# Two tiles of tokens through all heads, then the other two, in the last stage of a two-layer kernel

## The reference

```python
def _peer(h, wq, keys, u, v):                       # P_HEADS 8, P_TOPK 16, N_KEYS 128
    def block(xt):                                  # 128 tokens
        q = (xt @ wq).reshape(P_BLOCK, P_HEADS, 2, P_HALF)
        s = jnp.einsum('nhpd,hpkd->nhpk', q, keys)
        s1, i1 = lax.top_k(s[:, :, 0], P_TOPK)
        s2, i2 = lax.top_k(s[:, :, 1], P_TOPK)
        ...                                         # the 16 best of the 256 sums, idx = i1*128 + i2
        g = jax.nn.softmax(top_s.astype(jnp.float32), axis=-1)...
        act = jax.nn.gelu(jnp.einsum('nd,ned->ne', xt, u[idx]), approximate=False)
        return jnp.einsum('ne,ned->nd', g * act, v[idx])
```

## Time and profile before

| | |
|---|---|
| median of 3 runs | 4204.72 us (4201.19 to 4205.2) |
| the profiled execution | 4206.81 us, its span 4205.0 us |
| PE busy | 3455.8 us (82%) |
| DVE busy | 1977.0 us (47%) |
| POOL busy | 939.2 us (22%) |
| ACT busy | 657.9 us (16%) |
| moved by DMA | 1157.36 MB, mean 275 GB/s |
| gathers of the last stage | 512, first issued at 2838.4 us, last at 4170.2 us |

### The profile page before, as it was taken

The page is one execution under the profiler, slowest core; times in us unless marked ns, Lnnn a source line. Parts: engine busy times, 40 slices in busy tenths (PEclk is TensorE's granted clock), DMA queues, the critical chain, the costliest instruction groups (busy, mean ns, idle before and its releaser), DMA issues. The chain is left out here.

```text
span 4205.0 us, 37527 instructions
## 1 busy us (share of the span) xinstructions
PE 3455.8 (82%) x11876; PEld 1566.1 (37%) x11877; DVE 1977.0 (47%) x4086; ACT 657.9 (16%) x1532; POOL 939.2 (22%) x811
## 2 busy tenths in 40 slices
PE   7988998497999979998879655578888887887876
PEld 3345443332333323333254344444333333333332
DVE  5824223322332232232252264436666667667676
ACT  1011220000000000000021112212222222221212
POOL 2000000112221220121220040003444444444442
PEclk9999998698999989999989766689899999999998
DMA  9816333579989993888861000027999999999997
GB/s 331 287 72 229 111 102 112 205 277 411 367 347 363 386 412 121 311 333 337 311 233 61 6 1 0 1 80 300 421 418 417 419 408 413 413 409 421 411 421 333
DMA packets 194149, 1157.36 MB, mean 275 GB/s; under 512 B 25659, under 2 KB 27995, under 8 KB 74356
## 3 DMA queue, kind: packets, MB, share of 16 engines
q1 hardware_dynamic: 97140, 565.17, 34.6%
q0 software_dynamic: 80576, 564.05, 32.7%
q10 hardware_dynamic: 16320, 26.75, 2.1%
HBM read 1128.96 MB, written 48.68 MB: 280 GB/s over the span
## 5 line engine op out<-in xcount | busy, mean ns | idle before, releaser
L2167 POOL DMA_INDIRECT q_uv<-in_peer_uv,q_picks x512 | 576.3, 1126 | 1128.0 <-PE ps L2259 709.9
L1149 PE MATMUL ps<-wt,e_xT 128*64 128x512 f32 x3200 | 731.1, 611 | 99.6 <-DMA wt<-in_w_exp 98.7
L2462 DVE SCALAR_TENSOR_TENSOR mod<-q_uv,mix 128x1024 f32<-128x1024 f32 x512 | 627.3, 1225 | 391.1 <-DMA q_uv<-in_peer_uv,q_picks 386.7
L2259 PE MATMUL ps<-q_uv,q_dg 128*128 128x512 f32 x1024 | 512.3, 656 | 135.0 <-ACT q_dg L2336 135.0
L2259 PE MATMUL ps<-q_uv,tri 128*128 128x512 f32 x1024 | 474.0, 618 | 88.1 <-ACT tri L2336 88.0
L1129 POOL COPY wt<-e_land 128x2048 f32<-128x2048 f32 x124 | 237.6, 1916 | 1023.3 <-DMA e_land<-in_w_exp 1023.2
L1149 PEld LDWEIGHTS ps<-wt,e_xT 128*64 128x64 f32 x3200 | 237.7, 141 | 583.2 <-issue 432.2
L1149 PE MATMUL ps<-wt,e_aT 128*64 128x512 f32 x1600 | 356.0, 597 | 21.6 <-ACT e_aT L1202 21.6
L2259 PEld LDWEIGHTS ps<-q_uv,q_dg 128*128 128x128 f32 x1024 | 211.1, 211 | 427.2 <-issue 427.2
L2259 PEld LDWEIGHTS ps<-q_uv,tri 128*128 128x128 f32 x1024 | 198.1, 197 | 360.4 <-issue 360.4
L454 PE MATMUL ps<-hT,wt 128*128 128x512 f32 x640 | 285.0, 602 | 1.5 <-DVE wt L781 1.5
(11 more groups left out here) (439 smaller groups left out, 3483.2 us busy)
## 6 DMA issues: line engine op xcount, KB each, us to landing
wt<-in_w_exp SPq DMA_DIRECT2D x260, 1024.0 KB, 17.6
e_land<-in_w_exp SPq DMA_DIRECT2D x124, 1024.0 KB, 23.5
wt<-in_w_in_units SPq DMA_DIRECT2D x15, 2048.0 KB, 11.4
mod<-in_w_mod_units SPq DMA_DIRECT2D x48, 512.0 KB, 5.7
scratch_xs<-const_zeros SPq DMA_DIRECT2D x8, 2080.0 KB
mod<-in_w_ada_units SPq DMA_DIRECT2D x32, 512.0 KB, 6.1
p_ring<-in_w_in SPq DMA_DIRECT2D x7, 2048.0 KB, 9.6
e_xg<-scratch_xs ACTq DMA_DIRECT2D x104, 128.0 KB
```

The costliest lines, as they stand in the source:

```text
L1149: ins = nc.tensor.matmul(ps[64 * h:64 * h + 64, at, :], lhs[:, k % 4, 64 * (k // 4):64 * (k // 4) + 64], wt[:, u, a, h * W:(h + 1) * W], s ...
L2167: pool.indirect_dma_start(out=uv[:, n % NR, :, :].rearrange("p a d -> p (a d)"), out_offset=None, in_=A["peer_uv"], in_offset=bass.Indirec ...
L2259: last = nc.tensor.matmul(acc(t)[:, c, :], dg(n), uv[:, n % NR, 1, c * W:(c + 1) * W], start=fresh, stop=closing)
L2462: dve.scalar_tensor_tensor(junk[:, n % 2, :], uv[:, n % NR, 0, :], 1.0, mix[:, tile_of(k), :], ALU.mult, ALU.mult, accum_out=ap[:, k % 2, ...
```

## The change

The batches are taken in another order. Tiles 0 and 1 go through all eight heads (batches 0 to 15, the tile alternating), then tiles 2 and 3. There are now 16 rounds `v` of queries, each for one head and two tiles (256 tokens); the weights of head `v % 8` are loaded for each round, so every head's are read twice. A round is one stretch of 16 matmuls of 256 columns in bank 6 after gather 3 of each odd batch, and 4 score matmuls in bank 7 after gather 9. Round 0 is still done tile by tile; round 1 stands ahead of the gathers' matmuls, where tile 2's first queries were. Tiles 2 and 3 are transposed later (`columns`, in batches 2 and 4). Each tile has PSUM banks of its own; tile 3 takes tile 0's once it has been read (`s_tot`). `gather_sum`, `ysum` and `s_ev` are gone; `qT` and `sc` are half as large.

```diff
-ORDER = (0, 2, 1, 3)
+ORDER = (0, 1, 2, 3)
+PAIR = 2
+ROUNDS = PH * NT // PAIR
...
         def tile_of(k):
-            return ORDER[k % NT]
+            return PAIR * (k // (PAIR * PH)) + k % PAIR
 
         def acc(t):
-            return ps[:, 2 * min(t, 2):2 * min(t, 2) + 2, :]
+            return ps[:, 2 * (t % 3):2 * (t % 3) + 2, :]
...
-                for h in range(2, PH):
-                    sp.wait_ge(s_q, NT if h == 2 else q_done(h - 2, 1))
-                    sp.dma_start(wq[:, h % 2].rearrange("p k w -> p (k w)"), A["peer_wq_2_units"][h]).then_inc(s_wq[h % 2], 16)
-                    if h == 2:
+                for v in range(2, ROUNDS):
+                    sp.wait_ge(s_q, q_done(v - 2))
+                    sp.dma_start(wq[:, v % 2].rearrange("p k w -> p (k w)"), A["peer_wq_2_units"][v % PH]).then_inc(s_wq[v % 2], 16)
+                    if v == 2:
                         sp.wait_ge(s_h, NT)
                         sp.dma_start(ln2[:, 0, :], ...).then_inc(s_ln2, 16)
...
+                def queries(v):
+                    t = PAIR * (v // PH)
+                    pe.wait_ge(s_wq[v % 2], 16 * (v // 2 + 1))
+                    pe.wait_ge(s_h, t + PAIR)
+                    pe.wait_ge(s_qe, q_done(v - 1))
+                    if v in (3, 4):
+                        pe.wait_ge(s_tT, NT + 2 * v)
+                    for c in range(2):
+                        for k in range(KD):
+                            last = nc.tensor.matmul(ps[:, 6, c * PAIR * P:(c + 1) * PAIR * P], wq[:, v % 2, k, c * NK:(c + 1) * NK],
+                                                    hT[:, k, t * P:(t + PAIR) * P], start=(k == 0), stop=(k == KD - 1))
+                    last.then_inc(s_q, 1)
...
                 pe.wait_ge(s_mix, 2 * NT)
-                first_queries(2)
+                queries(1)
+                scores(1)
...
-                    if j == 0 and t >= 2 and k >= 2:
-                        pe.wait_ge(s_ev, k // 2)
+                    if j == 0 and k == PAIR * PH + 1:
+                        pe.wait_ge(s_tot, 1)
...
-                    if k == 0 and j == 3:
-                        first_queries(3)
-                    if h + 1 < PH and k % NT == 0 and j in (7, 13):
-                        queries(h + 1, int(j == 13))
-                    if h + 1 < PH and k % NT == 1 and j == 5:
-                        scores(h + 1)
+                    if k in (2, 4) and j == 5:
+                        columns(PAIR + k // 2 - 1)
+                    v = k // PAIR + 2
+                    if k % PAIR == 1 and v < ROUNDS:
+                        if j == 3:
+                            queries(v)
+                        if j == 9:
+                            scores(v)
...   (ScalarE, in batch k, after the diagonals of group g)
-                            if k % NT == 0 and g == 3:
-                                queries(h + 1, 0)
-                            if k % NT == 1 and g == 0:
-                                queries(h + 1, 1)
-                            if k % NT == 1 and g == 2:
-                                scores(h + 1)
+                        if k % PAIR == 1 and v < ROUNDS:
+                            if g == 1:
+                                queries(v)
+                            if g == 3:
+                                scores(v)
...   (VectorE)
-                def gather_sum(k):
-                    ...
-                        if j == 8 and 1 <= k <= last_head and tile_of(k - 1) >= 2:
-                            gather_sum(k - 1)
-                        if k > last_head and j in (6, 8, 10, 12, 14):
+                        if k - 1 in last_of and j in (6, 8, 10, 12, 14):
                             finish(k - 1, (j - 6) // 2)
```

More of the change, by code:

```diff
@@ L2104, in route_peer @@
         s_full, s_mix, s_h, s_q, s_qe, s_sc, s_se = (sem(n) for n in ("full", "mix", "h", "q", "qe", "sc", "se"))
[L2105 removed]
+        s_u, s_v, s_ge, s_w, s_dg, s_tot = (sem(n) for n in ("u", "v", "ge", "w", "dg", "tot"))
         s_uv = [sem(f"uv{i}") for i in range(NR)]
@@ L2114, in tile_of, with q_done, scores_done @@
         def tile_of(k):
-            return ORDER[k % NT]
+            return PAIR * (k // (PAIR * PH)) + k % PAIR
         def acc(t):
-            return ps[:, 2 * min(t, 2):2 * min(t, 2) + 2, :]
[L2122 to L2130, removed]
+            return ps[:, 2 * (t % 3):2 * (t % 3) + 2, :]
+        def q_done(v):
+            return PAIR + v
+        def scores_done(v):
+            return PAIR + v
+        last_of = {PAIR * PH * (t // PAIR + 1) - PAIR + t % PAIR: t for t in range(NT)}
         with nc.Block() as block:
@@ L2206, in first_queries @@
                     for c in range(2):
-                        last = nc.tensor.matmul(ps[:, 7, c * NK:(c + 1) * NK], qT[:, c, t * P:(t + 1) * P], keysT[:, c, :],
+                        last = nc.tensor.matmul(ps[:, 7, c * NK:(c + 1) * NK], qT[:, c, i * P:(i + 1) * P], keysT[:, c, :],
                                                 start=True, stop=True)
                     last.then_inc(s_sc, 1)
[L2211 to L2217, removed]
+                def queries(v):
[9 more added lines that the diff above has]
+                                                    hT[:, k, t * P:(t + PAIR) * P], start=(k == 0), stop=(k == KD - 1))
@@ L2218, in queries, with scores @@
                     last.then_inc(s_q, 1)
-                def scores(h):
-                    pe.wait_ge(s_qe, q_done(h, 1))
-                    for i, t in enumerate(ORDER):
+                def scores(v):
+                    pe.wait_ge(s_qe, q_done(v))
+                    pe.wait_ge(s_se, scores_done(v - 1))
+                    for i in range(PAIR):
                         for c in range(2):
-                            last = nc.tensor.matmul(ps[:, 6 + i // 2, (2 * (i % 2) + c) * NK:(2 * (i % 2) + c + 1) * NK],
-                                                    qT[:, c, t * P:(t + 1) * P], keysT[:, 2 * h + c, :], start=True, stop=True)
+                            last = nc.tensor.matmul(ps[:, 7, (2 * i + c) * NK:(2 * i + c + 1) * NK],
+                                                    qT[:, c, i * P:(i + 1) * P], keysT[:, 2 * (v % PH) + c, :], start=True, stop=True)
@@ L2227, in scores, with columns @@
                     last.then_inc(s_sc, 1)
+                def columns(i):
+                    t = ORDER[i]
+                    pe.wait_ge(s_h, i + 1)
+                    pe.wait_ge(s_tT, NT + 2 * i)
+                    pe.wait_ge(s_qe, q_done(i))
+                    pe.wait_ge(s_se, scores_done(i))
+                    for b in range(2):
+                        for k in range(4):
+                            last = nc.tensor.transpose(ps[:, 6 + b, k * P:(k + 1) * P],
+                                                       mix[:, t, (4 * b + k) * P:(4 * b + k + 1) * P], ident[:, :])
+                        last.then_inc(s_tm, 1)
@@ L2322, in _ @@
                 root(3)
-                first_queries(2)
+                queries(1)
+                scores(1)
                 exponentials(1)
                 for k in range(NBATCH):
-                    h = k // NT
+                    v = k // PAIR + 2
                     for g in range(BATCH // G):
@@ L2397, in choose @@
                 def choose(k, part):
-                    lists = [sc[:, (k // NT) % 2, k % NT, c, :] for c in range(2)]
+                    lists = [sc[:, (k // PAIR) % 2, k % PAIR, c, :] for c in range(2)]
                     settle()
                     if part == 0:
-                        dve.wait_ge(s_se, k + 1 if k < NT else scores_done(k // NT))
+                        dve.wait_ge(s_se, k + 1 if k < PAIR else scores_done(k // PAIR))
                         for c in range(2):
```

74 lines of the change are left out of this document (29 added, 45 removed).

## The result

The changed kernel takes 4211.8 us (median, 4207.16 to 4216.4), the kernel before 4202.57 us on the same chip (4198.59 to 4206.8); 18 runs each, ratio 1.0022 [1.0014, 1.0029]. So it is 9.2 us slower. I had forecast 0.5 us more: the result lies inside the stated range (4196 to 4222), just outside the forecast's own (4200 to 4211), and just beyond the 0.2% (8.4 us) that I had called "no change". The profiled execution took 4212.47 us, with a span of 4210.6 us.

A forecast was written before the change was run, and what follows sets the result against it. It took DMA transfers, full at 421 GB/s between query rounds, to bound the last stage. Terms +12.5 - 11.9 + 1.2 - 1.3 = +0.5 us gave 4207.3 us profiled, median 4205.2; range 4196 to 4222, the forecast's own 4200 to 4211.

The forecast's parts named there:

- step 2: Query bursts in the last stage: loads fill holes in the transfers, idle 8.0 us against 19.9, so -11.9 us.
- My signs: 46 us windows: over 415 GB/s around bursts ending with a load, about 405 around the last two; wrong at 400 or less.
- the second cause: Load and burst's hole add up instead of cancelling; sign: windows around bursts with a load at 400 GB/s or less.
- 1, loads: Last stage's full stretch: 12 weight loads instead of 6, ln2 leaves; net +5 MB at 2.49 us, +12.5 us.
- 3, start: Last stage's start: round 1's queries for two tiles replace tile 2's first, scores later by +1.2 us (bounds -1, +3).
- 4, tail: `gather_sum` goes; only its last instruction stands on the final chain: -1.3 us.
- 5, waits: Waits added for copied scores and queries: cost 0; 7 us if their cover went.
- on top of the hole: After each burst, load and first gathers share engines: 1.65 us more for 12 bursts, +19.8, 4225 us; chance 0.25.
- Evenly spaced bursts hurt no more: All 14 bursts' holes close, idle 0, -8.0 us: 4197 us, 4195 with the start's lower bound; chance 0.13.
- Short matmuls are slower: Query bursts: 16 uncovered weight loads make each 3 us longer, 43 us over 14, at most 4248 us; chance 0.04.

The follow-up runs named there:

- e10: Kernel before with only the changed kernel's start of the last stage, no load more: 4197.44 us beside 4203.85 us, ratio 0.999.
- e1: Kernel before with each query burst from batch 4 on cut into pieces, one behind each group of four gathers: 4206.08 us, before 4204.72 us, ratio 0.9999.
- e2: Changed kernel with each query burst cut into two halves 4 gathers apart: 4213.18 us, ratio to the kernel before 1.0016.
- e8: Kernel before with the second matmul of each gather cut from 512 columns to 2, output half wrong: 4198.6 us, ratio 0.999.
- e9: Kernel before with the second matmul of each gather left out, output half wrong: 4194.03 us, ratio 0.9981.
- e4: Changed kernel with loads from round 4 on issued 16 gathers later, between bursts: 4213.65 us, ratio to the kernel before 1.002.
- e3: Changed kernel without the second reading of query weights (8 loads of 1 MB gone, result not the reference's): 4194.2 us, ratio to the kernel before 0.9971.
- e5: Kernel before with seven more 1 MB loads, each issued as a round's first burst ends: 4218.43 us beside 4202.15 us, ratio 1.004.
- e6: Kernel before with seven more 1 MB loads, each in the middle between rounds of bursts: 4221.49 us beside 4202.15 us, ratio 1.0045.

## Why the prediction was right or wrong, step by step

The number fell into the stated range, but the mechanism on which the forecast stood failed (step 2): the range was wide enough for the result through its rivals, which took the same holes for real, and that is luck. My signs did not tell either: bursts with a load moved 421, 421, 401, 405 and 414 GB/s, partly as forecast and partly as in the second cause.

*1, loads (+12.5 us): right.* 6 loads more in the rounds gave 14.6 us, one MB less ahead of them 2.5 us back: 12.1 us.

*2, bursts (-11.9 us): this step failed.* I had written that TensorE's burst lets the ring run dry, and "a 1 MB load that starts as a burst ends fills the hole which the burst tears". Of the 11.9 us at most the 3.9 us that lie at the start came (dot product 64 is 6.3 us sooner, 2.5 us of that is the MB of ln2; with the changed start alone, in e10, 1.8 us were left); the 8.0 us of the rounds did not. Nothing was torn and nothing filled: the burst can be cut up (e1, e2), TensorE unloaded (e8, e9), the load moved (e4), left out (e3) or added at the burst or far from it (e5, e6), and a round takes 161 to 162 us plus about 2.5 us for each MB. The dips are real in the earlier trace rows, but I read them as time lost against the 421 GB/s of quiet windows. The trace of before has 16 landings for each gather, as many as there are DMA engines, and I take one to be each engine's. These show where the error is. Time of a gather's first landing (us from the span's start): us from it to the last landing:

```
before  3121.5: 2.02   3133.9: 2.99   3183.5: 4.05   3349.3: 5.07   3389.0: 5.16   3588.4: 1.15
after   2904.7: 1.88   3108.5: 3.02   3123.3: 4.01   3183.3: 7.19   3292.9: 6.40   3349.1: 8.55
```

Between 3121 and 3134 us, with two packets of the instruction queues at 3126.7 (queue 8) and 3127.0 (queue 14), the spread goes up by 1 us and stays. In a quiet stretch it grows to 5 us, while 421 GB/s are moved, and most of it is the very last landing (at 3349.3 us the 15th comes 2.4 us behind the first, the 16th 5.1): the other engines run ahead into the ring's slack, and one falls behind. When the ring is thin they wait for it, and the window shows a dip. In the changed kernel, with no dip for 400 us, the spread grew to over 6 us (over 8 around a load), and the dips then came without bursts. So a quiet window shows more than the lasting rate, and a dip shows what was run ahead.

What sets the lasting rate can be read from the last landings alone. In e9, where it is clearest, the last landing of a gather comes 2.485 us (median) behind that of the gather before. Besides the loads and stores, the delays of over 0.5 us from gather 64 on are 20 steps of 0.89 to 0.99 us, each beside a packet of queue 14:

```
gathers       64-128     128-192      192-256      256-320      320-384      384-448  448-511
steps at      74 98 118  140 163 184  207 230 250  274 294 318  339 360 384  406 426  450 470 498
```

64 x 2.485 = 159.0 us, three steps of 0.96 and a load of 2.5 are 164.4 us (measured 164.4 to 164.7), three steps without a load 161.9 (162.0), two steps 161.0 (161.1). So what a round takes beyond the bytes of its gathers and loads is two or three such steps. They stand beside 20 of the 29 packets of queue 14 in these rounds, which last only 0.325 us; beside the other 9 there is no delay. In the kernel before the steps are nearly the same, a few of them beside a packet of queue 8 alone (at 3435.6 and 3823.8 us). Its deepest window (3556 to 3604 us, 385 GB/s), which I had charged with 4.1 us, delays the last landings by 0.8 us beyond one load and one such step. So the late engine hardly waits through a burst. That its lateness makes the dips is argued, not shown, since the trace does not say which packets meet which of the 16 engines; why a packet of 0.325 us goes with a delay of almost 1 us stays open.

*3, start (+1.2 us): nearly right.* The scores are read 105.30 us after the stage's first DMA, before it was 105.18 us: +0.1 us. The burst took 10.16 us, more than my 9, but it started 92.6 us after the first DMA, where the records that it replaces had started at 97.5.

*4, tail (-1.3 us): not in this profile, but in three others.* The last sum went, but TensorE's last 16 records took 8.80 us at a granted clock of 0.81, beside 7.11 us before, and the tail from the last dot product on is 0.4 us longer (21.3 instead of 20.8 us). The profiles of e2, e3 and e4, which have the same tail, show 19.6 us, about the forecast saving, so that the 0.4 us may be this one execution's.

*5, waits (0): right.* One wait for scores in the rounds, 0.6 us.

With the part of step 2 that failed set to nothing the sum is 12.5 - 3.9 + 0.1 + 0.4 = +9.1 us, beside 9.2 us measured. All from the profiles it is 14.6 (rounds) - 6.3 (start) + 0.4 (tail) = 8.7 us; that the first sum comes nearer to the medians means nothing. The stage by itself is 8.7 us longer in the profiles (1441.9 instead of 1433.2 us from its first DMA to the end); the stages ahead of it 3.1 us shorter, though no line of them was changed.

The rivals: *on top of the hole* had the direction and the right price of a load (its +19.8 us, 4225 us in all, failed because it kept the holes as a loss). *Evenly spaced bursts hurt no more* saw idle 0, which the first 400 us did show, and it was worth nothing. *Short matmuls are slower* is excluded by 7.07 us. (So the trace also disagrees with the rule of the Trainium skill, "TensorE: Matmul & The Clock Gate", Part 3, in the kernel where it was to count: 32 records with as many weight loads in 7.07 us.) What I could have had from the earlier trace rows is a doubt: two holes of over 3 us and four of 1.0 to 1.8 us under bursts of equal length don't fit a cause that lies in the burst. And one sum would have decided it blind: time by round of 64 gathers, the last with no burst in it. One slip in the chances: a third of 0.13 is 0.04, where I added 0.06.

## What to carry to other kernels

Where a stretch is limited by DMA, compare times of equal pieces of work, with and without the suspected disturbance, before you turn dips of GB/s into us: a dip can be the other side of a quiet window that ran ahead. In such a stretch each MB costs its full 2.5 us wherever it is put, so moving a transfer pays only where the engines stand idle (here ahead of 2890 us), and reading weights twice costs all of the second reading. Instructions cost DMA time there, and far more than their bytes: 256 empty ones, 16 KB and so 0.04 us at 421 GB/s, cost 0.65 to 1.0 us on an engine that had nothing to do.

## What the runs showed of the hardware

- Instruction packets share the DMA engines. Queue 14's 8 KB packets, which more instructions on SP and on ScalarE both added to, cost 0.33 to 0.51 us of the stage's time each, on the mean. In e9 20 of 29 of them stood beside a delay of a gather's last landing by 0.89 to 0.99 us, the others beside none. Queue 8's 16 KB packets took an engine 1.07 us each, and 8 fewer of them, with fewer instructions on TensorE, saved nothing; why the two differ stays open.
- The 16 landings of a gather drift apart: in the changed kernel 1.9 us from first to last at 2905 us and 6.4 us at 3293 us, with 421 GB/s in the windows there, and 8.55 us beside a load at 3349 us.
- The granted clock followed TensorE's work: 0.94 in the window 3100 to 3850 us where it was busy 83%, 0.80 in e8 and 0.79 in e9 with half of the columns gone; the time of a round stayed.
